# Later transposes, other step orders and three sums moved to VectorE in an encoder layer

## The reference

```python
x = x + 0.5 * rmsnorm(swiglu(rmsnorm(x, g1), w1_gate, w1_up, w1_down), g1_post)
h = rmsnorm(x, g_mix);  z = h @ w_in            # [pool channels | q | k | v]
mix = concat(pool_mixer(u), dilated_window_attention(q, k, v)) @ w_out
x = x + rmsnorm(mix, g_mix_post)
x = x + 0.5 * rmsnorm(swiglu(rmsnorm(x, g2), w2_gate, w2_up, w2_down), g2_post)
# swiglu(h) = (silu(h @ w_gate) * (h @ w_up)) @ w_down, with 2752 inner channels
```

## Time and profile before

| what | value |
|---|---|
| time, median of 3 runs | 1754.96 us (1754.24 to 1759.48) |
| the profiled execution's own time | 1755.16 us |
| its span, first to last instruction | 1753.3 us |
| PE busy | 1709.8 us, 98% of the span |
| DVE busy | 1116.9 us, 64% |
| ACT busy | 712.0 us, 41% |
| POOL busy | 635.4 us, 36% |
| mean granted TensorE clock | 0.993 |

### The profile page before, as it was taken

One profiled execution on the slowest core, in us unless ns is written; L12 is line 12 of the kernel. 1 busy time (PEld: TensorE's weight loads), 2 busy tenths in 40 slices (PEclk: granted clock), 3 DMA queues, 4 the chain that ended last, 5 costly groups with the idle time before them and its releaser, 6 DMA issues.

```text
span 1753.3 us, 21676 instructions
## 1 busy us (share of the span) xinstructions
PE 1709.8 (98%) x7949; PEld 1406.1 (80%) x7949; DVE 1116.9 (64%) x1403; ACT 712.0 (41%) x1256; POOL 635.4 (36%) x494
## 2 busy tenths in 40 slices
PE   7999999999999999999999899999999999999997
PEld 6788888888888878887888677778888888888886
DVE  6776665655668774424556667877665656557877
ACT  6433333332444543434444556533333333244453
POOL 3465554543552111108010201346554544355111
PEclk9999999999999999999999999999999999999998
DMA  6132233233853445332110166322233233384362
GB/s 213 56 122 91 90 114 133 90 103 116 305 179 102 152 132 168 113 94 84 49 51 23 51 205 190 106 87 91 90 120 127 90 109 102 139 302 142 102 228 91
DMA packets 160985, 216.98 MB, mean 124 GB/s; under 512 B 12848, under 2 KB 99056, under 8 KB 160880
## 3 DMA queue, kind: packets, MB, share of 16 engines
q1 hardware_dynamic: 153136, 188.73, 33.7%
q10 hardware_dynamic: 6896, 24.19, 3.9%
q0 software_dynamic: 848, 2.69, 0.5%
HBM read 162.09 MB, written 52.95 MB: 123 GB/s over the span
## 4 chain that ended last, share of the span: by engine, by line
PE 83%; DVE 6%; issue 4%; ACT 3%; POOL 1%; DMA 1%; ACTq 0%; POOLq 0%; DVEq 0%
PE ps L1986 14%; PE ps L1987 14%; PE ps L1988 14%; PE ps L2049 7%; PE ps L2051 7%; PE ps L2050 7%; PE ps L2079 4%; PE ps L2081 4%; PE ps L2080 4%; PE ps L2189 2%; PE ps L2157 1%; PE ps L1871 1%; PE ps L2297 1%; POOL t_sum L1685 1%; PE ps L2172 1%
## 5 line engine op out<-in xcount | busy, mean ns | idle before, releaser
L1986 PE MATMUL ps<-xg,ring 128*128 128x512 f32 x1120 | 441.3, 394 | 2.9 <-DVE y L1227 2.7
L1987 PE MATMUL ps<-xg,ring 128*128 128x512 f32 x1120 | 438.7, 392 | 0.0
L1988 PE MATMUL ps<-xg,ring 128*128 128x512 f32 x1120 | 437.4, 391 | 0.0
L1986 PEld LDWEIGHTS ps<-xg,ring 128*128 128x128 f32 x1120 | 210.7, 188 | 49.9 <-issue 4.5
L1988 PEld LDWEIGHTS ps<-xg,ring 128*128 128x128 f32 x1120 | 210.7, 188 | 48.2
L1987 PEld LDWEIGHTS ps<-xg,ring 128*128 128x128 f32 x1120 | 210.9, 188 | 44.2
L2049 PE MATMUL ps<-ring 128*128 128x512 f32 x616 | 241.1, 391 | 1.4 <-DVE ring L1167 1.4
L2050 PE MATMUL ps<-ring 128*128 128x512 f32 x616 | 240.2, 390 | 0.0
L2051 PE MATMUL ps<-ring 128*128 128x512 f32 x616 | 240.2, 390 | 0.0
L685 ACT ACTIVATE ring<-t_sum 128x512 fp32r<-128x512 f32 x160 | 100.5, 630 | 294.1 <-PE ps L1988 162.0
L1174 DVE TENSOR_TENSOR ring<-raw,ring 128x1024 fp32r<-128x1024 f32 x64 | 84.3, 1317 | 144.2 <-ACT ring L714 130.1
(11 more groups left out here) (217 smaller groups left out, 2789.7 us busy)
## 6 DMA issues: line engine op xcount, KB each, us to landing
st_op<-hd_dram SPq DMA_DIRECT2D x154, 256.0 KB, 2.7
raw<-in_w_gate_dram SPq DMA_DIRECT2D x20, 1024.0 KB, 6.6
raw<-in_w_up_dram SPq DMA_DIRECT2D x20, 1024.0 KB, 5.5
raw<-in_w_in_dram SPq DMA_DIRECT2D x40, 512.0 KB, 3.8
hd_dram<-u_b SPq DMA_DIRECT2D x64, 256.0 KB, 6.4
wd<-in_w_down_dram SPq DMA_DIRECT2D x18, 768.0 KB, 7.2
hd_dram<-hst SPq DMA_DIRECT2D x48, 256.0 KB, 6.5
raw<-in_w_out_dram SPq DMA_DIRECT2D x24, 512.0 KB, 3.6
```

What stands on the lines that cost most here:

```text
L1986: pe.matmul(acc, hi[:, a, :], x_hi, start=(a == 0 and not more), stop=False, skip_group_check=more)
L1987: pe.matmul(acc, hi[:, a, :], x_lo, start=False, stop=False, skip_group_check=more)
L1988: mm = pe.matmul(acc, lo[:, a, :], x_hi, start=False, stop=(a == HALF_D - 1), skip_group_check=more)
```

## The change

1. The transposes of tiles 0 to 2 in the first down projection come a step later, as do the steps that take their high and low parts.
2. In `project_out` the third transpose comes at n = 20 instead of n = 21, and a turned tile's low part stands ahead of the other DVE steps of the same n.
3. `last_mixed` on DVE has the steps of tiles 5, 6, 7 in another order.
4. `first_steps` of both FFNs has another order on ACT and on DVE.
5. The last three of the five sums of h for the last pair run on DVE, behind its last step of `gate_up`. DVE waits for POOL's two sums first.

```diff
-TURN_AT, TURN_BANK, LO_AT, EVAC_AT = (13, 14, 16, 18), (4, 6, 4, 6), (14, 15, 17, 19), (11, 12, 12, 13)
+TURN_AT, TURN_BANK, LO_AT, EVAC_AT = (14, 15, 17, 18), (4, 6, 4, 6), (15, 16, 18, 19), (11, 12, 12, 13)
-OUT_NORM, OUT_TURN = (10, 12, 19, 20, 22), (12, 14, 21, 22)
+OUT_NORM, OUT_TURN = (10, 12, 19, 20, 22), (12, 14, 20, 22)
 # ScalarE, first_steps(p)
                 hi_g(p, 0)
+                x_hi(Q_FFN[p] + HT + 1, TURN2_BANK[1])
                 hi_g(p, 1)
-                x_hi(Q_FFN[p] + HT + 1, TURN2_BANK[1])
                 hi_g(p, 2)
...
                 hi_g(p, 5)
+                hi_g(p, 6)
                 s_hi(p, OP_S3)
-                hi_g(p, 6)
+                silu_tail(p, Z_T, 1)
+                s_hi(p, OP_S1)
                 hi_g(p, 7)
-                s_hi(p, OP_S1)
-                silu_tail(p, Z_T, 1)
                 hi_g(p, 8)
 # VectorE, first_steps(p)
                 lo_g(p, 0)
+                split(p, 0)
+                split(p, 1)
                 lo_g(p, 1)
+                lo_g(p, 2)
                 tail_times_up(p, Y_T, 0)
-                split(p, 0)
-                lo_g(p, 2)
-                split(p, 1)
                 lo_g(p, 3)
                 tail_times_up(p, Z_T, 0)
                 split(p, 2)
                 lo_g(p, 4)
                 split(p, 3)
                 lo_g(p, 5)
+                lo_g(p, 6)
+                s_lo(p, OP_S3)
                 for i in range(HT):
                     s_14(p, i)
-                lo_g(p, 6)
-                s_lo(p, OP_S3)
+                tail_times_up(p, Z_T, 1)
                 lo_g(p, 7)
                 s_lo(p, OP_S1)
-                tail_times_up(p, Z_T, 1)
 # VectorE, end of gate_up(p)
+                dve.wait_ge(u_done, 5 * PAIRS * (p + 1) - 3)
+                for x in (6, 7, 8):
+                    a, op, b = U_SUMS[x - 4]
+                    dve.wait_ge(h_done, 4 * GP * p + 4 * (GP - 1) + max(a, b) + 1)
+                    dve.tensor_tensor(h_operand(x), hst[:, a, :], hst[:, b, :], ALU.add if op == "+" else ALU.subtract)\
+                       .then_inc(u_done, 1)
 # VectorE, project_out: x_lo now stands ahead of NEW and NORM of the same n
+                    for i in range(HT):
+                        if n == OUT_TURN[i]:
+                            x_lo(Q_FFN[1] + i, 6, copied=True)
 # VectorE, last_mixed, behind evac_mix(2)
-                for i in range(EARLY, NT):
-                    scale_y(R_MIX + i, g_post_r)
-                    x_new(R_MIX + i)
+                scale_y(R_MIX + 5, g_post_r)
+                x_new(R_MIX + 5)
+                scale_y(R_MIX + 6, g_post_r)
+                x_new(R_MIX + 6)
                 lo_tail(1, Z_T)
-                for i in range(EARLY, NT):
-                    x_norm(Q_FFN[1] + i, g_pre_r)
+                scale_y(R_MIX + 7, g_post_r)
+                x_norm(Q_FFN[1] + 5, g_pre_r)
+                x_new(R_MIX + 7)
+                x_norm(Q_FFN[1] + 6, g_pre_r)
+                x_norm(Q_FFN[1] + 7, g_pre_r)
 # GpSimd, h_sums(p, j)
-                for x, (a, op, b) in enumerate(U_SUMS):
+                for x, (a, op, b) in enumerate(U_SUMS[:2] if j == GP - 1 else U_SUMS):
```

More of the change, by code:

```diff
@@ L1581, in project_out @@
                             x_norm(Q_FFN[1] + i, g_pre_r)
-                        if i < HT and n == OUT_TURN[i]:
-                            x_lo(Q_FFN[1] + i, 6, copied=True)
                 lo_tail(1, X_T)
```

## The result

The changed kernel takes 1744.60 us (median of 5 runs, 1741.27 to 1746.79) against 1754.96 (1754.24 to 1762.06): ratio 0.9937, 95% interval 0.9917 to 0.9957. It is faster by 10.4 us. The forecast was 1745.5, in a range of 1740.5 to 1749.5. The profiled execution took 1744.6 us with a span of 1742.8.

The account below looks back on a forecast made before the run. PE works in 98% of the span, so only its idle time and slow matmuls can be won. Gains 4.4 + 2.1 + 0.8 + 0.9 + 1.6 = 9.8, less 0.1, take 1755.2 to 1745.5 us; range 1740.5 to 1749.5.

Parts of the forecast that it names:

- Parts 1 and 2: First down projection: turn's wait and slow clock shrink, gain 4.4 us; front of first FFN: two waits go, gain 2.1.
- The stand of VectorE at tail_times_up(Z, 1): Both FFN fronts: rival that VectorE's DMA wait outlasts its 3.2 us cover before m = 4; 1751.1 us, chance 0.10.
- Part 3: Entry to both down projections: three sums on VectorE let lo_d(2) run at full speed; gain 0.4 us each, 0.8.
- The rival "slower": Down projection entries: the three sums and lo_d(2) halves take 1.7 us each, delaying PE; 1759.5 us, chance 0.04.
- Part 4: Output projection: wait at n = 22 goes, new wait of 2.0 us at n = 20; gain 0.9 us.
- Part 5: Between mixer and second FFN: several waits replaced by one 4.0 us silu wait and a slow stretch; gain 1.6 us.
- the late case: Before second FFN: GpSimd's tile 5 factor waits for a 1.2 us VectorE instruction; sum 1745.5 us, without it 1745.0.
- more slow stretches: Attention stage and n = 20: rival of one or two more slow-clock stretches; 1747.1 to 1748.7 us, chance 0.18.
- 7.2 - 4.0 - 1.6: Mixer to second FFN: 7.2 us lost before, less 4.0 new idle time and 1.6 slow clock; 1.6 gained.
- the clock did fall behind the long wait: Second FFN's front: rival that the clock stays at 2.4 GHz behind the 4.0 us idle time; 1743.9, chance 0.12.
- The gate through sq2(7): Second FFN's front: x_new(7), square, then silu hold PE; rival that they do not, 1739.8 us, chance 0.10.

Follow-up runs that it names:

- the part alone: The kernel before with only the first down projection's transposes and their low parts a step later: 1749.86 us.
- experiment 4: Changed kernel plus 34 transposes of the identity on PE ahead of the second FFN's tail product Z: 1741.91 us, ratio 0.9929.
- Experiments 2: Changed kernel with VectorE's old order in `last_mixed`, all else kept: 1741.08 us, ratio 0.9921.
- experiment 5: The kernel before with one part of the change, one run each: turns 1749.86 us, sums 1754.36, both `first_steps` orders 1747.23.
- 7: Side by side on one chip: changed kernel 1745.86 us; with old `last_mixed` 1740.45; with earlier silu, third turn at n = 21, x_new(7) ahead of all norms 1740.29.
- experiment 1: Changed kernel with ScalarE's first silu of the second FFN ahead of the square of tile 7: 1741.97 us, ratio 0.9931.
- experiment 3: Changed kernel with the output projection's third transpose back at n = 21 and x_lo(2) earlier on VectorE: 1743.65 us, ratio 0.9938.

## Why the prediction was right

The measured time lies 0.9 us under the forecast, and the mechanism of each part was seen as it was told. That the sum fits so closely is in part luck, since the attention stage alone scatters by 1 to 2 us.

**Parts 1 and 2** held to 0.1 us. The turn waits 0.33 where 0.5 was forecast, and no slow stretch follows; the dates give 4.35 for 4.4, in the changed kernel and in the part alone. The first front gave 2.2 for 2.1. The stand of VectorE at tail_times_up(Z, 1) never reached PE: in the first FFN the last s_lo(S1) is done at 62.9 and product m = 4 starts at 65.86, in the second at 1144.6 and 1147.61. Both have 3.0 us of cover, where 3.2 was forecast.

**Part 3** (the sums) held: 0.4 for each FFN. The forecast took 0.6 for a sum, and three took 1.88 together. lo_d's half took 0.68 with no GpSimd sum beside it, and 1.77 beside GpSimd's sums. The rival "slower" fell with it. The rule of the Trainium skill ("SBUF — State Buffer", "Who interferes with whom"), that a VectorE instruction with two SBUF inputs and a GpSimd instruction that reads SBUF exclude each other for a whole instruction, fits both figures.

**Part 4** held: 0.83 for 0.9, with the new wait at 1.85 for 2.0. The forecast's own terms, 1092.9 + 0.8 + 8.4, give 1102.1 where it writes 1102.3, so its gain would have been 1.1.

**Part 5** held in its result, 1.78 for 1.6, by the chain that was named: one wait for the silu, one slow stretch, nothing behind it. The wait was 3.66 in the row (3.9 in true cost) for 4.0, the slow stretch 1.66 (experiment 4) for 1.6. GpSimd's column for tile 5 took 1.41 beside VectorE, and x_norm(5) waited 0.44 for it, where the late case had 0.5.

**What was not forecast** is 0.7 us gained in the attention stage, where the forecast named only the risk of more slow stretches. The parts sum to 9.9 for 9.7 forecast, and the stage brings the difference of the profiles to 10.6. That stage scatters by itself: from the last matmul on w_in to step 8 of the output projection, two executions of the kernel with the old `last_mixed` differ by 2.2 us and two of the changed one by 1.1, with two or three slow stretches in each. Of the 2.2 us 1.5 is one slow stretch behind the wait at step 2 (see the last section).

**What the forecast did not weigh** is that within part 5 the new order of `last_mixed` is a loss. It booked that order with the rest as one bill of 7.2 - 4.0 - 1.6. Its own numbers would have shown it: without the order, PE keeps the 1.75 and 0.46 at tile 5 and the silu, and loses nothing else, 2.2 instead of 5.6. Experiments 2, 5 and 7 measured 3.3, 3.3 (5.05 against 1.78) and 3.6 for it. The reading that led past it was right, that x_new(7) is the gate; the step from there to "then do not put a norm ahead of it" was not made.

The rivals: the clock did fall behind the long wait; behind the 1.9 at n = 20 it did not in the profiled execution, but did in experiment 1. So more or fewer slow stretches are in part a matter of the execution. The gate through sq2(7) held.

## What to carry to other kernels

Before an order is changed for the instruction that PE waits for first, follow the next product's chain through every engine. Here a norm was pulled ahead of a sum whose square, on a third engine, stood ahead of the silu that PE needs next: two waits of 1.8 together saved, one of 3.7 and a slow clock paid. A wait removed upstream is kept only as far as the slowest list downstream moves with it (experiment 3 kept none of its 2.0 us). Where one stage scatters more than the effect, compare the dates behind it: two traces of a kernel agree to 0.2 us from step 8 on, while their spans differ by 0.6 to 3.1. Split a change with several reorderings into a bill for each: the sum came out right to 1 us and still held a part that cost 3.3.

## What the runs showed of the hardware

- Equal waits of PE do not have equal consequences for its clock. Behind 1.85 to 1.87 us at n = 20 it stayed at 2.4 GHz in both traces of the changed kernel, in both with the old order of `last_mixed` and in experiment 4, and fell to 1.2 in experiment 1. Behind 2.79 at n = 22 it stayed in the kernel before and fell in all three runs of experiment 5. Behind 2.0 at product m = 1 it fell before and stayed in the runs with the turns alone and the sums alone. In those two, a slow stretch had begun at 1090 and 1095. What decides it stays open.
- At one place the 13 traces do divide by the wait. At step 2 of the output projection PE waits for VectorE's low parts (`mlo`). Where the wait was 1.94 to 2.82 us, a slow stretch began within 0.7 us of its end. That is so in all seven traces with such a wait, among them the kernel before and both of the changed kernel, and PE then took 22.0 to 22.1 us to step 8. In the other six traces it was 0.48 to 1.70 us, no slow stretch began there, and PE took 20.6. PE has shorter waits just ahead of this one, so the wait alone need not be the cause.
- A slow stretch in these places lasted 3.4 us and cost 1.66 in the second FFN's front (experiment 4), and 1.5 behind step 2 of the output projection. After two waits of 1.24 and 3.73 it lasted 6.8.
- The table load for the silu takes 1.28 us, and the silu starts 1.29 behind the load's start, so its whole price is 1.3. In experiment 1 a square behind the silu needed no load of its own.
